# Starting the delta rule's keys, gates, key products and inversion inside the even layer's input projection

## The reference, cut to what matters

```python
p = rms_norm(x, norm_g) @ w_in
qkv_a, beta_l, alpha_l, z_a, q_b, k_b, v_b, z_b = split_cols(p, EVEN_SIZES)
qkv_a = jax.nn.silu(causal_depthwise_conv(qkv_a, conv_w)).astype(F32)
...
q = l2norm(q) * (Dh ** -0.5)
k = l2norm(k)
beta = jax.nn.sigmoid(beta_logit)
g = -jnp.exp(a_log) * jax.nn.softplus(alpha_logit + dt_bias)
...
gc = jnp.cumsum(to_chunks(g[..., None])[..., 0], axis=-1)
decay = jnp.exp(jnp.where(causal, gc[..., :, None] - gc[..., None, :], -jnp.inf))
l_mat = jnp.where(strict, jnp.einsum('bnhid,bnhjd->bnhij', k_beta, kc) * decay, 0.0)
m_mat = jnp.eye(CHUNK, dtype=F32) + l_mat
sol = lax.linalg.triangular_solve(m_mat, rhs, left_side=True, lower=True, unit_diagonal=True)
```

## Time and profile before

| | us |
|---|---|
| time, median of 3 runs (lowest, highest) | 1633.26 (1632.69, 1633.31) |
| the profiled execution: its own time | 1631.34 |
| its span, first to last instruction | 1629.6 |
| PE busy | 1301.2 (80%) |
| DVE busy | 911.0 (56%) |
| ACT busy | 441.9 (27%) |
| POOL busy | 335.7 (21%) |

### The profile page before, as it was taken

The page is one execution under the profiler, slowest core; times in us unless marked ns, Lnnn a source line. Parts: engine busy times, 40 slices in busy tenths (PEclk is TensorE's granted clock), DMA queues, the critical chain, the costliest instruction groups (busy, mean ns, idle before and its releaser), DMA issues. The chain is left out here.

```text
span 1629.6 us, 20032 instructions
## 1 busy us (share of the span) xinstructions
PE 1301.2 (80%) x8242; PEld 1079.6 (66%) x8242; DVE 911.0 (56%) x1211; ACT 441.9 (27%) x638; POOL 335.7 (21%) x172
## 2 busy tenths in 40 slices
PE   3999999967673595993999799999531688988498
PEld 3688888835563584873788688888221478888387
DVE  5277620116857646415897555673579667564831
ACT  5222321241332125005342122231543321312300
POOL 2233212201633005202231111121210310000320
PEclk9999999987887597995999899999765576999699
DMA  5212222030000003135233141612000000010513
GB/s 171 40 39 63 58 78 78 26 142 21 1 1 1 2 1 118 63 126 159 83 101 104 46 129 35 187 54 89 13 1 1 1 1 1 2 52 2 177 59 126
DMA packets 117987, 99.84 MB, mean 61 GB/s; under 512 B 37064, under 2 KB 102600, under 8 KB 117768
## 3 DMA queue, kind: packets, MB, share of 16 engines
q1 hardware_dynamic: 104552, 80.60, 16.8%
q10 hardware_dynamic: 13344, 17.96, 3.4%
HBM read 73.38 MB, written 23.46 MB: 59 GB/s over the span
## 5 line engine op out<-in xcount | busy, mean ns | idle before, releaser
L167 PE MATMUL banks<-xt_lo,w_hi 128*128 128x512 f32 x816 | 320.3, 393 | 7.5 <-POOL w_lo L457 7.3
L168 PE MATMUL banks<-xt_hi,w_lo 128*128 128x512 f32 x816 | 318.3, 390 | 0.0
L169 PE MATMUL banks<-xt_hi,w_hi 128*128 128x512 f32 x816 | 318.0, 390 | 0.0
L457 POOL TENSOR_TENSOR w_lo<-features,w_hi 128x1024 fp32r<-128x1024 f32 x55 | 149.4, 2719 | 473.3 <-ACT w_hi L466 473.3
L167 PEld LDWEIGHTS banks<-xt_lo,w_hi 128*128 128x128 f32 x816 | 153.7, 188 | 42.5 <-POOL w_lo L457 8.5
L169 PEld LDWEIGHTS banks<-xt_hi,w_hi 128*128 128x128 f32 x816 | 153.6, 188 | 31.9
L168 PEld LDWEIGHTS banks<-xt_hi,w_lo 128*128 128x128 f32 x816 | 153.7, 188 | 31.4
L506 ACT ACTIVATE temporaries<-banks 128x1024 f32<-128x1024 f32 x45 | 54.0, 1201 | 331.0 <-PE banks L169 316.6
L1414 DVE TENSOR_TENSOR temporaries<-temporaries,banks 128x1024 f32<-128x1024 f32 x16 | 19.6, 1222 | 115.7 <-PE banks L169 106.9
L785 PE MATMUL banks<-features,big 32*32 32x32 f32 (+1 forms) x640 | 30.1, 233 | 59.8 <-DVE features L745 57.3
L574 DVE SCALAR_TENSOR_TENSOR temporaries<-features,temporaries 128x1024 f32<-128x1024 f32 x8 | 16.5, 2057 | 109.1 <-ACT features L523 109.1
(11 more groups left out here) (430 smaller groups left out, 2649.4 us busy)
## 6 DMA issues: line engine op xcount, KB each, us to landing
features<-in_even_w_in SPq DMA_DIRECT2D x26, 512.0 KB, 3.9
features<-in_odd_w_in SPq DMA_DIRECT2D x25, 512.0 KB, 4.6
features<-in_x SPq DMA_DIRECT2D x8, 512.0 KB, 4.6
even_gates<-temporaries ACTq DMA_DIRECT2D x8, 512.0 KB, 2.7
features<-even_gates SPq DMA_DIRECT2D x8, 512.0 KB, 7.3
features<-in_even_w_out SPq DMA_DIRECT2D x8, 512.0 KB, 3.4
temporaries<-in_x SPq DMA_DIRECT2D x8, 512.0 KB, 4.1
h_between_layers<-temporaries SPq DMA_DIRECT2D x8, 512.0 KB, 4.4
```

The lines of the kernel that those rows point to most:

```text
L167: nc.tensor.matmul(out, w[0], x[1], start=start, stop=False)
L168: nc.tensor.matmul(out, w[1], x[0], start=False, stop=False)
L169: return nc.tensor.matmul(out, w[0], x[0], start=False, stop=stop)
L457: nc.gpsimd.tensor_tensor(wl[n % 2], wr[n % NW], wh[n % 2].bitcast(F32), ALU.subtract).then_inc(low, 1)
```

## The change

Blocks change order: the four k blocks come first (0 to 3), then q (4 to 7) and v (8 to 11), all eight gate blocks (12 to 19), kb and vb (20, 21; now written to HBM and fetched again, since their place in SBUF is taken), and qb (22 to 25) last. Three programs now run beside the projection, merged by due number (`together`). `gdn_front` holds the norm of k, the gates, and for each chunk the sums of g, the product of keys, clip, exponential, mask and `n`. `gdn_invert` is the inversion, due numbers 13 to 18.8. PE now also runs steps between the halves of a block, and DVE, ACT and POOL run steps due by n-0.5 ahead of their part of block n. `gdn_gates` and the separate inversion are gone, "eq" has 9 blocks, and `gdn_chunks` keeps only what needs q and v: sums of g again, transposes, the product with q, one mask, the scaling of q. The inversion uses two banks and a smaller scratch in all its calls; its products of 2048 elements are cut in two.

```diff
--- before.py
+++ after.py
                 else:
                     for h in range(2):
+                        if h:
+                            aside.upto(n - 0.5)
                         hs = slice(h * 512, (h + 1) * 512)
...
             for n in range(NB):
+                aside.upto(n - 0.5)
                 pool.wait_ge(high, n + 1)
                 nc.gpsimd.tensor_tensor(wl[n % 2], wr[n % NW], wh[n % 2].bitcast(F32), ALU.subtract).then_inc(low, 1)
                 aside.upto(n)
...
-                if kind == "turned":
+                if kind in ("turned", "spill"):
                     spill(n)
...
+        yield pace(35)
+        pool.wait_ge(v_ready, 1)
         nc.gpsimd.memset(x11[0:32, :, 32:64], 0.0).then_inc(zeroed, 1)
...
+        for c, n, r0, r1 in ((0, 8, 0, H), (8, 16, 0, 8), (8, 16, 8, H)):
...
+def gdn_invert(co):
+
+    program = invert(co, "gi", co.at(A_F[4], (NT * HG, P)), GDN_INVERT, low_bank=4, pace=lambda t: 13 + t / 10, ready=(co.n_sliced, 16), free=(co.n_made, NT))
...
+def gdn_front(co, a_log, dt_bias):
...
+    def scalar(act):
+        def square(n):
+            act.wait_ge(co.finished, n + 1)
+            if n >= 3:
+                act.wait_ge(summed, n - 2)
+            nc.scalar.activation(sq[n % 3], k[:, n, :], ACT.Square).then_inc(squared, 1)
+
+        yield 2.5
+        square(0)
...
+        for c in range(NT):
+            yield 8.5 + 0.5 * c
+            act.wait_ge(clipped, c + 1)
+            if c:
+                act.wait_ge(masked, c)
+            nc.scalar.activation(dt2, dt, ACT.Exp).then_inc(decayed, 1)
+            if c % 2 == 0 and c:
+                act.wait_ge(n_made, c)
+                for b in range(4):
+                    own = slice(32 * b, 32 * b + 32)
+                    nc.scalar.activation(blocks[own, HG * (c - 2):HG * c, :], n_st[own, HG * (c - 2):HG * c, 32 * b:32 * b + 32], ACT.Copy).then_inc(sliced, 1)
...
+    def tensor(pe):
+        for n in range(HG):
+            yield (3, 4, 5, 5.5)[n]
+            pe.wait_ge(squared, n + 1)
...
+            yield 7 + 0.5 * (n // 2)
+            if n == 0:
+                pe.wait_ge(low_r, 4)
+            if n >= 2:
+                pe.wait_ge(normed, n - 1)
...
+        def cumulate(c):
+            if c >= 2:
+                pe.wait_ge(clipped, c - 1)
+            for h in range(HG):
+                s = c * HG + h
+                last = nc.tensor.matmul(cum(c)[:, h, :], g[:, s:s + 1].to_broadcast([P, P]), upper, start=True, stop=True)
+            last.then_inc(cumulated, 1)
+
+        yield 8
+        pe.wait_ge(normed, HG)
+        cumulate(0)
+        for c in range(NT):
+            yield 8.5 + 0.5 * c
+            ct = slice(c * P, (c + 1) * P)
+            if c:
+                pe.wait_ge(n_made, c)
+            for h in range(HG):
+                s = c * HG + h
+                nc.tensor.matmul(bank(5)[:, h, :], k[:, h, ct], k[:, h, ct], start=True, stop=True)
+                last = nc.tensor.matmul(bank(6)[:, h, :], beta[:, s:s + 1].to_broadcast([P, P]), ident, start=True, stop=True)
+            last.then_inc(products, 1)
+            if c + 1 < NT:
+                cumulate(c + 1)
...
+        for n in range(HG):
+            yield 7.5 + 0.5 * (n // 2)
+            dve.wait_ge(spread, n + 1)
+            v = k[:, n, :].rearrange("p (h t) -> p h t", h=2)
+            nc.vector.tensor_tensor(v, v, co.ps[:, 4 + 2 * (n % 2):6 + 2 * (n % 2), :], ALU.mult).then_inc(normed, 1)
...
+        def clip(c):
+            dve.wait_ge(cumulated, c + 1)
+            if c:
+                dve.wait_ge(decayed, c)
+            for h in range(HG):
+                s = c * HG + h
+                last = nc.vector.tensor_scalar(dt[:, h, :], cum(c)[:, h, :], gc[:, s:s + 1], 0.0, ALU.subtract, ALU.min)
+            last.then_inc(clipped, 1)
+
+        yield 8.5
+        clip(0)
+        for c in range(NT):
+            yield 9 + 0.5 * c
+            dve.wait_ge(products, c + 1)
+            dve.wait_ge(masked, c + 1)
+            link(nc.vector.tensor_tensor(tn, bank(5), ds, ALU.mult))
+            nc.vector.tensor_tensor(n_st[:, c * HG:(c + 1) * HG, :], tn, bank(6), ALU.mult).then_inc(n_made, 1)
+            if c + 1 < NT:
+                clip(c + 1)
+
+    def gpsimd(pool):
+        for c in range(NT):
+            yield 8.5 + 0.5 * c
+            pool.wait_ge(decayed, c + 1)
+            if c:
+                pool.wait_ge(n_made, c)
+            nc.gpsimd.tensor_tensor(ds, dt2, strict, ALU.mult).then_inc(masked, 1)
...
-                if c:
-                    pe.wait_ge(qkd, c)
-                    pe.wait_ge(n_made, c)
+                if c >= 2:
+                    pe.wait_ge(qkd, c - 1)
                 for h in range(HG):
-                    s = c * HG + h
-                    nc.tensor.matmul(bank(1)[:, h, :], k[:, h, ct], q[:, h, ct], start=True, stop=True)
-                    nc.tensor.matmul(bank(0)[:, h, :], k[:, h, ct], k[:, h, ct], start=True, stop=True)
-                    last = nc.tensor.matmul(bank(3)[:, h, :], beta[:, s:s + 1].to_broadcast([P, P]), ident, start=True, stop=True)
+                    last = nc.tensor.matmul(bank(c % 2)[:, h, :], k[:, h, ct], q[:, h, ct], start=True, stop=True)
                 last.then_inc(products, 1)
                 if c + 1 < NT:
                     decays_and_turns(c + 1)
...
-                dve.wait_ge(products, c + 1)
-                dve.wait_ge(masked, 2 * c + 1)
-                nc.vector.tensor_tensor(qk_st[:, cs, :], bank(1), di, ALU.mult).then_inc(qkd, 1)
-                dve.wait_ge(masked, 2 * c + 2)
-                if c:
-                    dve.wait_ge(n_made, c)
-                link(nc.vector.tensor_tensor(tn, bank(0), ds, ALU.mult))
-                nc.vector.tensor_tensor(n_st[:, cs, :], tn, bank(3), ALU.mult).then_inc(n_made, 1)
                 if c + 1 < NT:
                     clip_and_turn(c + 1)
+                dve.wait_ge(products, c + 1)
+                dve.wait_ge(masked, c + 1)
+                nc.vector.tensor_tensor(qk_st[:, cs, :], bank(c % 2), di, ALU.mult).then_inc(qkd, 1)
...
-    blocks = [(EVEN["q"] + P * b, "conv", q[b]) for b in range(WB)]
-    blocks += [(EVEN["k"] + P * b, "conv", k[b]) for b in range(WB)]
+    kb, vb = co.at(A_BIG + 1088, (T,)), co.at(A_BIG + 64, (T,))
+    blocks = [(EVEN["k"] + P * b, "conv", k[b]) for b in range(WB)]
+    blocks += [(EVEN["q"] + P * b, "conv", q[b]) for b in range(WB)]
     blocks += [(EVEN["v"] + P * b, "conv", v[b]) for b in range(WB)]
     blocks += [(EVEN["za"] + P * b, "gate", zg[b]) for b in range(WB)]
+    blocks += [(EVEN["zb"] + P * b, "gate", zg[WB + b]) for b in range(WB)]
+    blocks += [(EVEN["kb"], "spill", kvb[0]), (EVEN["vb"], "spill", kvb[1])]
     blocks += [(EVEN["qb"] + P * b, "plain", qb[b]) for b in range(WB)]
-    blocks += [(EVEN["kb"], "plain", kb), (EVEN["vb"], "plain", vb)]
-    blocks += [(EVEN["zb"] + P * b, "gate", zg[WB + b]) for b in range(WB)]
...
-    project(co, "ep", a["even_w_in"][0], blocks, conv_w=a["gdn_conv_w"][0], small=small, also=(gains_in, 16 * len(gains)), beside=bias_beside(co, a["rel_bias"], s5_early(co, a)))
-
-    norm_blocks(co, "eq", [(x_, 64, qn, None) for x_ in qb] + [(kb, 64, kn, None)] + [(x_, 128, 1.0, None) for x_ in q + k], 0,
-                fetch=[(zb[b], zg[WB + b]) for b in range(WB)] + [(za[b], zg[b]) for b in range(WB)])
+    project(co, "ep", a["even_w_in"][0], blocks, conv_w=a["gdn_conv_w"][0], small=small, also=(gains_in, 16 * len(gains)), 
+            beside=together(bias_beside(co, a["rel_bias"], s5_early(co, a)), gdn_front(co, a["gdn_a_log"][0], a["gdn_dt_bias"][0]), gdn_invert(co)))
+
+    norm_blocks(co, "eq", [(x_, 64, qn, None) for x_ in qb] + [(kb, 64, kn, None)] + [(x_, 128, 1.0, None) for x_ in q], 0, late=(kb, kvb[0]),
+                fetch=[(vb, kvb[1])] + [(zb[b], zg[WB + b]) for b in range(WB)] + [(za[b], zg[b]) for b in range(WB)])
     swa_prepare(co, a["swa_sinks"][0])
     swa_attend(co, co.at(A_F[6], (WB, T)))
-    gdn_gates(co, a["gdn_a_log"][0], a["gdn_dt_bias"][0])
     gdn_chunks(co)
-    side_by_side(co, invert(co, "gi", store_slot(co, 0), GDN_INVERT))
     gdn_state(co)
```

More of the change, by code:

```diff
@@ L304, in in_turn, with together, of, steps_of @@
         due[i] = next(steps[i], NEVER)
+def together(*programs):
+    def of(name):
+        mine = [program[name] for program in programs if name in program]
+        def steps_of(eng):
+            steps = [program(eng) for program in mine]
+            due = [next(step, NEVER) for step in steps]
+            while min(due, default=NEVER) < NEVER:
+                i = due.index(min(due))
+                yield due[i]
+                due[i] = next(steps[i], NEVER)
+        return steps_of
+    return {name: of(name) for name in ("sync", "tensor", "gpsimd", "scalar", "vector")}
 def side_by_side(co, *programs):
@@ L492, in _ @@
             for n, (col, kind, dst) in enumerate(blocks):
+                aside.upto(n - 0.5)
```

(20 more changed lines are left out.)

354 lines of the change are left out of this document (194 added, 160 removed).

## The result

The changed kernel takes 1735.05 us (median; 1730.76 to 1739.74) against 1633.28 for the one before: a ratio of 1.0613, 95% interval 1.0575 to 1.0651. I had forecast 1700 with a range of 1678 to 1722. The direction was right, and the loss, 102 us, is one and a half times the 67 I had worked out. Of the 31 executions of the kernel before on record, 26 took 1630 to 1637 us and five took 1653 to 1665, four of them with a recorded mean clock of 0.861 to 0.867 for the usual 0.878 to 0.883.

A forecast was written before the change was run, and what follows sets the result against it. PE was taken to bound the projection, DVE's chain the gates, chunk and inversion stages. Added projection time +168 and savings −101 gave net +67, so 1700 us on the median of 1633.26; range 1678 to 1722.

The forecast's parts named there:

- Ends of blocks 9 to 11: Projection, blocks 9, 10, 11: PE waits for `n`, then the next low part, 20.1 us each; +60.
- End of block 8: Projection: first sums wait 10.6 us for the multiplied keys, then 5.5 until block 9's low part; +18.
- End of block 12: Projection, behind a gate block: 5.7 us until the last `n`, then 5.3 through the low part; +11.
- The middles: Inside blocks 9 to 12: 8 products and 4 sums each, plus 1.3 us lost per low-clock restart; +16.5.
- Block 17: Projection: its low part waits behind a clearing that needs the substitution's last transpose, PE idle; +21.4.
- Blocks 17 to 19, merging: Projection: PE's own merging about 15 us, waits of 4.3, 1.3 and 3.7, and 3.4 for the clock; +28.
- Before block 9: Projection: sums, spreads, bias and gate sums 8.4 us on PE, and 5.1 of short waits; +13.5.
- Sum of the projection: All added terms: +168, the projection growing from 298.6 to about 467 us, some 105 of it PE idle.
- the first rival: Steps fit beside the projection's blocks, PE finding inputs ready, only about 48 us of own work added: 1580; chance 0.03.
- What it takes away: Savings outside the projection, in gates, inversion, chunk and norm stages and the projection's end: together −101.
- The odd layer's inversions: Odd layer: its inversions get smaller pieces; +1 (0 to 2).
- The clock rival: Projection: waits restart PE at half clock, perhaps seven blocks low throughout, +58, 1757; chance of over +25: 0.06.

The follow-up runs named there:

- the odd form undone: The changed kernel with the odd layer's two inversions in their earlier form (own areas, products of 2048, x placed as soon as ready): 1721.31 us.
- The masks' experiment: The changed kernel with GpSimd's masks one place later, behind the next block's low part instead of ahead of it: 1704.96 us.
- The loads' experiment: The changed kernel with the odd layer's small loads issued beside blocks 21 and 23 instead of 14 to 18: 1738.31 us.
- the form alone: The kernel before with only its odd layer's inversions in the new form: 1674.79 us, ratio 1.0227.
- the new due numbers and the new odd form: The changed kernel with the same work at other due numbers, some steps reordered and the guard split, odd inversions kept in the new form: 1586.25 us.

## Why the prediction was right in sign and wrong in size

Term by term, from the profiled execution. A difference of 4 to 5 us in the whole projection is within what executions differ by: with the odd form undone, which changes nothing there, it ended 4.6 us earlier. The waits repeat within 0.5 us.

- *Ends of blocks 9 to 11* (+60): 20.6, 20.1 and 20.6 between the blocks. Right; 9.59 and 5.52 for the forecast 9.5 and 5.5. The masks' experiment took the second half away and left the first, as the lists say.
- *End of block 8* (+18): 18.1 (10.53 and 5.52). *End of block 12* (+11): 11.1. Right.
- *The middles* (+16.5): blocks 9 to 12 lasted 15.9, 16.4, 15.4 and 16.1 for 11.04, so 19.6. A little too low; behind the waits 7 to 12 of a block's matmuls came every 0.43 us, where 1.3 us lost stands for 6.
- *Block 17* (+21.4): 26.5. The substitution was the bound, as forecast, but the 4.3 us by which a gate block's transfer delayed it were missing. I had seen such a transfer wait in the trace of before and set it at nothing, since PE did not wait for it there. The loads' experiment shows the 4.3: 22.2 without them.
- *Blocks 17 to 19, merging* (+28): from the start of block 17 to that of block 20, 67.4 us for three blocks of 10.9, so 34.8; the waits were as forecast (4.52, 1.38, 3.88), the rest is clock.
- *Before block 9* (+13.5): block 8 ended at 175.77 for 156.12, so 19.7. The waits were 3.31 and 3.44, 6.8 for the forecast 5.1, and the clock fell already behind them, which I had priced at nothing.
- *Sum of the projection* (+168): 191.8. Its waits are 112.7, of which I had 105; its busy time grew by 79.2, of which I had 63. The forecast 63 are 48 of own work, as the first rival has it, and 15 of clock; measured were 41.9 and 37.3. So the clock was 22 us short, and an own work that I had 6 too high hides a part of that. **The failed step in the projection** is the rate of 1.3 us for each restart from the earlier trace rows: it is one case's 2.7 us at the low level, here that lasted 5.4 and 6.1 us behind the short waits, and I had priced no restart ahead of block 9.
- *What it takes away* (−101): −106.3. The chunk stage gave 23.3 for 22 and the inversion stage 56.9 for 57.6. Norm stage, end of the projection, attention and gates together gave 26.1 for 21.8; no run tells what made the other 4.
- *The odd layer's inversions* (+1, bounds 0 to 2): **this term failed most.** The profiled execution lost 18.7 in the head states and 4.4 behind them, and the form alone costs the kernel before 41. Of the 18.7, 11.7 stand at and behind the wait of 2.52 us that the new form gives PE, and 7.4 in the second scan. Undoing the form gave back 14 on the median, so of the 23 some 9 have no shown cause. I had counted the added instructions on DVE, 6 × 3.1 against 18.3 us, and priced neither that wait nor the clock of a stage in which PE is busy 138.0 of 152.9 us. Both bounds came from DVE's rows, in a stage whose bound is PE.

The restart behind the wait of 3.44 us shows how much more one can cost than 1.3 us:

```profile
157.98 0.79 PE L1011 MATMUL banks<-k_rows_lo,one_hot 128*128 128x512 f32 x1 [3.44 <-DVE k_rows_lo L1068]
...
163.69 0.63 PE L169 MATMUL banks<-xt_hi,w_hi 128*128 128x512 f32 x1
164.12 0.43 PE L167 MATMUL banks<-xt_lo,w_hi 128*128 128x512 f32 x1
```

From 157.98 to 164.12 the matmuls come every 0.43 us, then every 0.23: 14 matmuls, so 2.9 us lost, and by the same working 2.6 behind the wait of 3.31.

So the lower rival, the steps fitting beside the blocks, did not hold for this order, for the reason given: order in the lists, not free time. That is shown, since the same work in another order, with the guard split, gains 48 us where this one loses 102. The clock rival was wrong in form (no block ran low throughout; the clock came back each time, later than in the earlier trace rows) and right in direction.

What stays open: what decides between the levels of the head-state stage. The same list of PE's instructions took 171.6 in one kernel and 195.7 in another whose head-state stage has the same program and only starts 12 us earlier. The second scan took 38.5 or 45.8 us with nothing of the inversion beside it. The form shifts the odds, as the times with and without it show; it does not explain two levels for one program. No experiment here fixes it, and what made the rest behind the head states 4.4 us longer is open too.

## What to carry to other kernels

Work placed beside a busy engine by its position in the lists is free only if every step finds its inputs made in an earlier round; for each such step, walk back from its wait and see whether the chain passes through the block that the busy engine has just finished. Shift the consumer one round later rather than making the chain faster. And when a shared helper is reshaped for one caller, price it again at each other caller, against the engine that bounds the stage there.

## What the runs showed of the hardware that was not expected

TensorE was at the lower level already behind a wait of 3.3 us. The eight instructions of a sum of squares took 0.64 us right behind a block, and 1.08 behind the wait at 134.82 shown above:

```profile
124.78 0.64 PE L996 MATMUL banks<-features,constants 128*32 128x256 f32 x8
```

The fall need not come at once. In the kernel with the loads later the same sums took 0.64 us behind the same wait, and the matmuls slowed from one in 0.23 us to one in 0.43 only from 135.74 on, for 3.3 us:

```profile
134.37 0.64 PE L996 MATMUL banks<-features,constants 128*32 128x256 f32 x8 [3.32 <-ACT features L942]
```

In the odd layer, after 2.52 us, the clock fell within 3 us of work; in the kernel before, with 0.45 at that place, it stayed up. Three transposes (L2380, before L2212) and twelve products (L2390, L2222) show it:

```profile
1483.38 1.20 PE L815 MATMUL banks<-features,big 32*32 32x32 f32 x64 [2.52 <-ACT features L793]
...
1487.42 0.85 PE L2380 MATMUL banks<-constants,features 128*128 128x128 f32 x3
1488.19 2.24 PE L2390 MATMUL banks<-features 64*128 64x128 f32 x12
```

```profile
1396.28 1.20 PE L785 MATMUL banks<-features,big 32*32 32x32 f32 x64 [0.45 <-ACT features L764]
...
1399.25 0.50 PE L2212 MATMUL banks<-constants,features 128*128 128x128 f32 x3
1399.67 1.26 PE L2222 MATMUL banks<-features 64*128 64x128 f32 x12
```

0.85 and 2.24 against 0.50 and 1.26, a factor of 1.7 to 1.8: the two levels. With the new due numbers and the new odd form the wait there is 2.54 us; the clock fell too, but was back at the twelve products:

```profile
1338.95 1.20 PE L815 MATMUL banks<-features,big 32*32 32x32 f32 x64 [2.54 <-ACT features L793]
...
1341.85 1.81 PE L2463 MATMUL banks<-temporaries,big 128*128 128x64 f32 x8
...
1343.97 1.26 PE L2416 MATMUL banks<-features 64*128 64x128 f32 x12
```

So a wait's length alone does not tell what it costs: this one cost the second part of the stage 3.8 us in one kernel, 11.7 in two and 21.0 in three. Nor does it tell the level behind it. In the attention of the kernel before, eight matmuls took 1.97 us behind a wait of 1.92 and 1.09 behind one of 2.88:

```profile
407.90 1.97 PE L1258 MATMUL banks<-constants,temporaries 128*128 128x128 f32 x8 [1.92 <-POOL temporaries L1320]
...
421.85 1.09 PE L1258 MATMUL banks<-constants,temporaries 128*128 128x128 f32 x8 [2.88 <-POOL temporaries L1320]
```

The head-state stage, 1383 matmuls, took between 153 and 196 us in these kernels, and 172 or 196 with the very same program in the stage.
